# Running four families of recurrence products as pairs in the two column halves of TensorE's array

## What is computed

```python
def _rwkv7_mixer(h, ...):
    r_h, k_h, v_h, a_h, w_h = heads(r), heads(k_mod), heads(v), heads(a), heads(decay)
    def step(state, inp):
        r_t, w_t, k_t, v_t, ka_t, kb_t = inp
        sa = jnp.einsum('bhvk,bhk->bhv', state, ka_t)
        state = (state * w_t[:, :, None, :] + sa[..., None] * kb_t[:, :, None, :]
                 + v_t[..., None] * k_t[:, :, None, :])
        return state, jnp.einsum('bhvk,bhk->bhv', state, r_t)
    _, y = lax.scan(step, state0, (tm(r_h), tm(w_h), tm(k_h), tm(v_h), tm(-kk), tm(kk * a_h)))
    yn = _groupnorm_heads(y, gn_w, gn_b, RWKV_GN_EPS)
    ...
    return ((yn + bonus) * g.astype(jnp.float32)).astype(h.dtype) @ w_out
```

## Time and profile before

| what | value |
|---|---|
| timed runs | 3888.39, 3895.55, 3895.81 us; median 3895.55 |
| profiled execution | span 3887.7 us from the first to the last instruction; the profile gives no other time for it |
| the three runs above that span | 0.7, 7.9 and 8.1 us |
| TensorE busy (3840.0 us) | 99% of the span |
| VectorE, GpSimd, ScalarE busy | 53%, 35%, 18% |
| mean granted TensorE clock | 0.997 of full speed |
| the recurrence, first to last product | 3242.9 to 3400.7 us, 157.8 us |

### The profile page before, as it was taken

One profiled execution on the slowest core, in us unless ns is written; L12 is line 12 of the kernel. 1 busy time (PEld: TensorE's weight loads), 2 busy tenths in 40 slices (PEclk: granted clock), 3 DMA queues, 4 the chain that ended last, 5 costly groups with the idle time before them and its releaser, 6 DMA issues.

```text
span 3887.7 us, 47138 instructions
## 1 busy us (share of the span) xinstructions
PE 3840.0 (99%) x18558; PEld 3007.9 (77%) x18558; DVE 2047.1 (53%) x3808; ACT 691.3 (18%) x1509; POOL 1362.4 (35%) x1181
## 2 busy tenths in 40 slices
PE   9999999999999999999999999999999999999999
PEld 4468888755888886888845888888888647858888
DVE  4568778458777764433246633244333655553333
ACT  3321110125111102100025200010001232320000
POOL 0015444203444441444404444444443043034443
PEclk9999999999999999999999999999999999999999
DMA  3125454320354441222220222222222242122222
GB/s 127 54 71 201 168 184 158 105 87 23 136 191 177 147 170 68 87 87 84 88 83 12 76 87 87 84 79 98 87 82 93 65 131 66 33 72 87 87 86 77
DMA packets 134891, 387.43 MB, mean 100 GB/s; under 512 B 39088, under 2 KB 47408, under 8 KB 125328
## 3 DMA queue, kind: packets, MB, share of 16 engines
q1 hardware_dynamic: 117344, 301.03, 23.5%
q10 hardware_dynamic: 16272, 79.90, 5.4%
q0 software_dynamic: 1056, 3.49, 0.3%
HBM read 375.26 MB, written 8.39 MB: 99 GB/s over the span
## 4 chain that ended last, share of the span: by engine, by line
PE 93%; DVE 4%; DMA 1%; ACT 1%; issue 0%; POOL 0%; SPq 0%; ACTq 0%; DVEq 0%; POOLq 0%
PE bank L1028 92%; DVE area_b L2700 1%; DVE normed L2641 1%; DMA weight_ring<-in_weights_dram 1%; PE bank L1687 0%; PE bank L1583 0%; DVE normed L2761 0%; PE bank L1872 0%; DVE area_b L2770 0%; DVE area_a L2771 0%; DMA residual<-in_x_dram 0%; DVE rstd L2660 0%; ACT area_b L2022 0%; DVE area_b L3388 0%; POOL area_b L1009 0%
## 5 line engine op out<-in xcount | busy, mean ns | idle before, releaser
L1028 PE MATMUL bank<-normed,weight_ring 128*128 128x256 f32 (+2 forms) x3584 | 959.2, 427 | 4.1 <-ACT normed L2022 1.6
L1028 PEld LDWEIGHTS bank<-normed,weight_ring 128*128 128x128 f32 (+1 forms) x3584 | 658.6, 188 | 270.3 <-issue 194.0
L1028 PE MATMUL bank<-area_b,weight_ring 128*128 128x256 f32 (+3 forms) x2144 | 525.7, 417 | 7.0 <-POOL area_b L1016 2.6
L1028 PEld LDWEIGHTS bank<-area_b,weight_ring 128*128 128x128 f32 (+2 forms) x2144 | 379.3, 184 | 116.9 <-issue 65.9
L918 POOL TENSOR_TENSOR area_d<-weight_ring 128x512 f32<-128x512 f32 (+1 forms) x112 | 142.1, 1269 | 856.4 <-PE bank L1028 727.6
L1028 PE MATMUL bank<-area_b,area_d 128*128 128x256 f32 x1688 | 383.7, 379 | 0.2 <-DVE area_b L2680 0.2
L1028 PE MATMUL bank<-area_a,weight_ring 128*128 128x256 f32 (+1 forms) x1448 | 375.2, 412 | 2.7 <-DMA weight_ring<-in_weights_dram 2.3
L918 POOL TENSOR_TENSOR area_b<-weight_ring 128x512 f32<-128x512 f32 (+1 forms) x102 | 129.1, 1266 | 686.3 <-PE bank L1028 641.7
L1028 PE MATMUL bank<-area_b 128*128 128x256 f32 (+2 forms) x1656 | 362.9, 375 | 0.1
L1028 PEld LDWEIGHTS bank<-area_b,area_d 128*128 128x128 f32 x1688 | 320.5, 190 | 44.8 <-DVE area_b L2680 1.3
L1028 PEld LDWEIGHTS bank<-area_b 128*128 128x128 f32 (+1 forms) x1656 | 298.4, 190 | 56.5 <-issue 13.7
(11 more groups left out here) (384 smaller groups left out, 4946.9 us busy)
## 6 DMA issues: line engine op xcount, KB each, us to landing
weight_ring<-in_weights_dram SPq DMA_DIRECT2D x435, 512.0 KB, 4.6
area_b<-in_weights_dram ACTq DMA_DIRECT2D x48, 1024.0 KB, 4.9
weight_ring<-in_weights_dram SPq DMA_DIRECT2D x24, 1024.0 KB, 4.7
area_b<-in_weights_dram ACTq DMA_DIRECT2D x48, 512.0 KB, 6.0
weight_ring<-in_weights_dram SPq DMA_DIRECT2D x43, 384.0 KB, 4.3
weight_ring<-in_weights_dram SPq DMA_DIRECT2D x29, 256.0 KB, 3.8
weight_ring<-in_weights_dram SPq DMA_DIRECT2D x38, 128.0 KB, 4.0
low_scratch<-area_d ACTq DMA_DIRECT2D x16, 256.0 KB, 2.2
```

Of the source, the lines that this page charges most:

```text
L1028: i = pe.matmul(out, lhsT, rhs, start=start, stop=stop)
```

## The change

Products whose stationary operand had 128 columns are each split into two with 64 columns, one for each column half, and the two are issued one behind the other. A new helper `column_tiles` gives the output partitions and the stationary columns of the two. This is done in `z` (both terms), `u`, `token_values` and the `START` term of `y`. In `y` the two halves' products are also issued in turn, and the wait for `U` now stands ahead of all of a pair's `U` products.

```diff
+            def column_tiles(c=0):
+                return [(slice(o, o + 64), slice(c * P + o, c * P + o + 64)) for o in (0, 64)]
...
             def token_values(i):
...
-                    mm(pbank(m)[:, b * P:(b + 1) * P], A[:, 16 + 2 * g + b, chunk(c)], const("centre"), True, True,
-                       product_full if b else None)
+                    for r, (rows, tokens) in enumerate(column_tiles(c)):
+                        mm(pbank(m)[rows, b * P:(b + 1) * P], A[:, 16 + 2 * g + b, tokens], const("centre"), True, True,
+                           product_full if b and r else None)
...
             def z(i):
...
                     if c:
-                        mm(sbank(s)[:, b * P:(b + 1) * P], B[:, 2 * g + b, chunk(c)], START[i % 2][:, b, :], True, False)
+                        for rows, tokens in column_tiles(c):
+                            mm(sbank(s)[rows, b * P:(b + 1) * P], B[:, 2 * g + b, tokens], START[i % 2][:, b, :], True, False)
                     for half in range(2):
                         e = 2 * half + b
                         o = b * P + 64 * half
-                        mm(sbank(s)[:, o:o + 64], VALUES_TO_Z[i % 2][:, e * P:(e + 1) * P], tok[:, 4 + b, 64 * half:64 * half + 64],
-                           c == 0, c == 0 or half == 1, small_full if b and half else None)
+                        for r, (rows, tokens) in enumerate(column_tiles(e)):
+                            mm(sbank(s)[rows, o:o + 64], VALUES_TO_Z[i % 2][:, tokens], tok[:, 4 + b, 64 * half:64 * half + 64],
+                               c == 0, c == 0 or half == 1, small_full if b and half and r else None)
...
             def u(i):
...
-                    mm(sbank(s)[:, 64 * e:64 * e + 64], INVERSE_T[i % 2][:, e * P:(e + 1) * P], Z[:, 2 * (e % 2) + e // 2, :],
-                       True, True, small_full if e == 3 else None)
+                    for r, (rows, tokens) in enumerate(column_tiles(e)):
+                        mm(sbank(s)[rows, 64 * e:64 * e + 64], INVERSE_T[i % 2][:, tokens], Z[:, 2 * (e % 2) + e // 2, :],
+                           True, True, small_full if e == 3 and r else None)
...
             def y(i):
...
-                    if c:
-                        mm(pbank(m)[:, q], START[i % 2][:, b, :], A[:, 2 * g + b, chunk(c)], True, False)
-                    for half in range(2):
-                        e, rows = 2 * half + b, slice(64 * half, 64 * half + 64)
+                    halves = slice(0, 64), slice(64, P)
+                    for rows in halves if c else ():
+                        mm(pbank(m)[rows, q], START[i % 2][:, b, rows], A[:, 2 * g + b, chunk(c)], True, False)
+                    for half, rows in enumerate(halves):
                         to_y_keys = TO_Y[i % 2][half][:, (2 + b) * P:(3 + b) * P]
                         mm(pbank(m)[rows, q], tok[:, 4 + b, rows], to_y_keys, c == 0, False)
-                        if b == 0 and half == 0:
-                            sdone(pe, RW_SMALL["u", i])
-                        mm(pbank(m)[rows, q], U[:, e, :], TO_Y[i % 2][half][:, q], False, True,
+                    if b == 0:
+                        sdone(pe, RW_SMALL["u", i])
+                    for half, rows in enumerate(halves):
+                        mm(pbank(m)[rows, q], U[:, 2 * half + b, :], TO_Y[i % 2][half][:, q], False, True,
                            product_full if b and half else None)
```

## The result

The changed kernel takes 3871.28 us (median of four runs, 3868.64 to 3873.74) against 3893.25 for the kernel before (median of four, 3888.39 to 3895.81): ratio 0.9944, 95% interval 0.9932 to 0.9956. The forecast was 3872, 23.4 us less than before; the medians are 22.0 us apart.

The account below looks back on a forecast made before the run. TensorE, busy 99% of the span, was taken to bound the kernel. Gains of 6.9 (u), 6.9 (z), 6.1 (y), 3.0 (token_values) and 0.7 (last step), less a 0.2 wait, gave 23.4 us: 3895.55 to 3872, range 3862 to 3876.

Parts of the forecast that it names:

- TensorE bounds the stage, and what goes from it goes from the time: Recurrence, 157.8 us: TensorE busy all 10.41 us of step 4, so time taken from its families is time of the kernel.
- A pair costs one pass, with 64 moving columns: u and z: two half-width passes take the time of one; u 0.61 us for 1.04, 6.9 us each family.
- the rival that ends slower: Split products: pairs don't run side by side where both halves stream the same data; 12 us more, 3908, chance 0.06.
- 128 moving columns gain only by the shape: START in y, and token_values: pairing gives nothing by itself, fewer tile shape changes do; y 6.1 us, token_values 3.0.
- The rival that the shape changes stay: y and token_values: START still pays for a change, or passes wait in PSUM; 9.1 us go, 3881, chance 0.05.
- The last step: y(15), waiting for U: START and tok of the first heads fit into the wait; 1.43 us for 2.11, 0.7 gained.
- The wait in step 2: inverse32 in step 2 waits for VectorE's copy of LOW32 behind two memsets of START: 0.2 us, once.
- the rival that VectorE comes late: Copies of LOW32 hold up inverse32 in every step: z's 6.9 us lost, 16.5 left, 3879, chance 0.05.
- The sum: Whole kernel: 23.6 - 0.2 = 23.4 us less, from the median 3895.55 to 3872.

Follow-up runs that it names:

- the parts: Four kernels, each the kernel before with only u, z, y or token_values changed: recurrence 6.70, 6.55, 7.00 and 3.09 us less than 157.79.

## Why the prediction was right, point by point

- *TensorE bounds the stage, and what goes from it goes from the time.* Right: 8.80 us of a step's 8.80 are busy, and the parts add up to 23.34 us.
- *A pair costs one pass, with 64 moving columns.* Right: u 0.62 (0.61 forecast), z 0.62 and 1.06 (0.61 and 1.05). The form that no row of before showed, both halves streaming the same data, pairs like the others. With it falls the rival that ends slower. The Trainium skill (TensorE: Matmul & The Clock Gate, Part 3, The mechanism) has weight loads overlap matmuls in flight only where the row groups differ; the trace disagrees for the two column halves, as u has 16 passes of 64 columns, all over the same 128 rows, in 0.62 us.
- *128 moving columns gain only by the shape.* Right: y 1.36 (1.37), state with token_values 1.00 (1.01). That a change of shape has a price of its own is shown without any pairing by the two START products put together. The rival that the shape changes stay is out.
- *The last step.* Right in kind, a little too large: from the end of u (3382.48) to the next stage 1.54 us, forecast 1.43, before 2.11; 0.57 us gained, not 0.7. The copy of U ends 0.46 us after u, where the forecast had 0.45; what follows it took 1.08 us where the forecast had 0.98 (3382.94 to 3384.02):

```profile
3381.79 0.69 PE L1028 MATMUL bank<-area_d,normed 128*64 128x64 f32 x16 [0.57 <-ACT area_d L2032]
...
3382.52 0.42 DVE L3537 COPY area_d<-bank 128x256 f32<-128x256 f32 x1 [1.90 <-PE bank L1028]
```

- *The wait in step 2.* Right: 0.26 us for 0.2, once, and it goes when VectorE's memsets go. No later step has such a wait, so the rival that VectorE comes late is out. The prediction's reading of the earlier trace rows, that the first link on another engine stands before the last step's u, leaves out the first step, where TensorE waits for VectorE too; the two kernels don't differ there.
- *The sum.* 23.4 us forecast (23.25 without the rounding of its terms), 23.3 in the stage, 22.0 between the medians of the runs. That the median fell within 1 us of the forecast 3872 is luck: the start of the recurrence alone moves by 9.5 us between profiles, and a fourth run took the median of the kernel before from 3895.55 to 3893.25. The span alone would have misled by 6.7 us, all of it ahead of the recurrence.

## What to carry to other kernels

From start to start, in these traces an fp32 pass that loads 128 columns takes 0.11 us whether it streams 64 (u before) or 128 (token_values before); one that loads 64 takes 0.06 with 64 streamed (u after) and 0.11 with 128 (y). So where a product streams fewer columns than it loads, splitting it over the two column halves of the array shortens it; where it streams as many, it doesn't. Other sizes and other types were not measured. Count the changes of tile shape in the order as well: products of one shape put side by side save some 0.1 us on either side of a change, without being split. And issue the two halves of a pair as neighbours.

## What the runs showed of the hardware that was not expected

- Products in the two column halves don't start in the order of issue alone. Four passes apart in the order they still nearly pair (u 0.66 us); eight apart the later half runs beside the earlier one only for its last four passes (0.90); neighbours take 0.62.
- A stage's beginning can fall into a stretch of lower granted clock in one profile and not in the next (0.52 over 14 us against 1.00 for the same kernel). It came to 5.4 us, more than the effect that was looked for.
